# A hybrid decoder step with 64 routed experts: the row lists of the passes turned inside their tiles, and the weights of the last three passes asked for in another order

## The reference

```
scores = sigmoid(h @ w_router)                      # 64 experts in 8 groups
eidx   = the 8 best experts out of the 4 best groups, per row
w      = scores[eidx] / sum * 2.5
routed = sum over the 8 experts e of a row:  w_e * ( silu(h @ w_gate_e) * (h @ w_up_e) ) @ w_down_e
shared = (silu(h @ w_gate_sh) * (h @ w_up_sh)) @ w_down_sh
x      = x + routed + shared,   then a final norm
```

## Time and profile before

| what | value |
|---|---|
| time, median of 3 runs (lowest to highest) | 1099.09 us (1098.98 to 1101.42) |
| the profiled execution | 1099.3 us, of which the span shown by the profile is 1097.5 us |
| PE busy | 934.3 us, 85% of the span |
| PE weight loads busy | 440.3 us, 40% |
| DVE, ACT, POOL busy | 404.1, 202.2, 242.0 us (37%, 18%, 22%) |
| bytes moved by DMA | 289.66 MB, 264 GB/s over the span |
| mean granted TensorE clock | 0.946 of full speed |

### The profile page before, as it was taken

One profiled execution on the slowest core, in us unless ns is written; L12 is line 12 of the kernel. 1 busy time (PEld: TensorE's weight loads), 2 busy tenths in 40 slices (PEclk: granted clock), 3 DMA queues, 4 the chain that ended last, 5 costly groups with the idle time before them and its releaser, 6 DMA issues.

```text
span 1097.5 us, 13692 instructions
## 1 busy us (share of the span) xinstructions
PE 934.3 (85%) x4773; PEld 440.3 (40%) x4773; DVE 404.1 (37%) x975; ACT 202.2 (18%) x415; POOL 242.0 (22%) x301
## 2 busy tenths in 40 slices
PE   4979987997988889799899897899797979999784
PEld 3564555465534544333333332333232324333231
DVE  5957447857873652123111111111111111111116
ACT  6050031141213131111111110111110111111103
POOL 1910029002300166102111211112111210222012
PEclk9989998998999899899899998999898999999988
DMA  9720120231226118899999999999999999999945
GB/s 325 304 77 5 74 78 0 77 90 70 47 79 231 46 55 346 359 377 385 394 381 384 385 389 392 376 381 374 370 394 382 372 374 376 359 339 388 381 147 195
DMA packets 66421, 289.66 MB, mean 264 GB/s; under 512 B 17291, under 2 KB 18539, under 8 KB 41392
## 3 DMA queue, kind: packets, MB, share of 16 engines
q1 hardware_dynamic: 45376, 250.21, 57.7%
q0 software_dynamic: 13232, 35.04, 12.2%
q10 hardware_dynamic: 7744, 3.53, 1.2%
HBM read 257.14 MB, written 41.18 MB: 272 GB/s over the span
## 4 chain that ended last, share of the span: by engine, by line
PE 47%; issue 29%; DVE 13%; ACT 5%; DMA 4%; ACTq 1%; SPq 0%; POOL 0%; DVEq 0%; POOLq 0%
PE bank L998 24%; PE bank L1944 21%; DVE arena L1592 3%; DVE arena L698 2%; PE bank L1036 2%; DMA prm<-expert_lists 1%; DVE arena L800 1%; ACT arena L1265 1%; DMA sum_rows<-arena,xs 1%; ACT arena L1252 1%; DVE bb L720 1%; DMA qkv_samples<-arena 1%; DVE arena L1923 1%; DMA arena<-in_x_prompt 1%; DVE arena L1905 1%
## 5 line engine op out<-in xcount | busy, mean ns | idle before, releaser
L998 PE MATMUL bank<-arena 128*32 128x512 f32 (+6 forms) x2930 | 539.7, 601 | 82.2 <-issue 52.9
L998 PEld LDWEIGHTS bank<-arena 128*32 128x32 f32 (+3 forms) x2930 | 198.3, 132 | 391.1 <-issue 376.4
L1944 PE MATMUL bank<-arena 128*128 128x512 f32 (+9 forms) x1208 | 309.2, 444 | 32.7 <-ACT arena L1549 8.5
L1944 PEld LDWEIGHTS bank<-arena 128*128 128x128 f32 (+4 forms) x1208 | 173.0, 191 | 162.3 <-issue 128.8
L465 POOL DMA_INDIRECT arena<-h_rows,xs x42 | 43.6, 1039 | 466.7 <-DVE bb L720 455.3
L698 DVE SCALAR_TENSOR_TENSOR arena<-arena,xs,bank 128x256 f32<-128x256 f32 x42 | 27.7, 660 | 312.1 <-issue 271.5
L695 DVE COPY arena<-bank 128x512 f32<-128x512 f32 x41 | 28.4, 692 | 179.1 <-PE bank L998 174.6
L554 ACT ACTIVATE arena<-bank 128x256 f32<-128x256 f32 x42 | 16.1, 383 | 328.7 <-PE bank L998 284.2
L474 POOL DMA_INDIRECT sum_rows<-arena,xs x41 | 64.6, 1576 | 53.4 <-DVE arena L695 30.6
L1592 DVE TENSOR_TENSOR arena<-arena 64x512 f32<-64x512 f32 (+8 forms) x79 | 68.3, 865 | 6.5 <-DMA arena<-o_samples 3.8
L484 POOL DMA_INDIRECT expert_lists<-arena,ncim x40 | 39.8, 994 | 91.4 <-issue 87.7
(11 more groups left out here) (231 smaller groups left out, 529.1 us busy)
## 6 DMA issues: line engine op xcount, KB each, us to landing
arena<-in_w_gate_e SPq DMA_DIRECT2D x64, 1024.0 KB, 18.4
arena<-in_w_up_e SPq DMA_DIRECT2D x64, 1024.0 KB, 34.5
arena<-in_w_down_e SPq DMA_DIRECT2D x64, 1024.0 KB, 33.8
arena<-in_w_in SPq DMA_DIRECT2D x5, 2048.0 KB, 9.0
expert_lists<-arena SPq DMA_DIRECT2D x1, 8482.5 KB, 28.9
arena<-in_x_prompt SPq DMA_DIRECT2D x8, 512.0 KB, 5.9
arena<-in_w_out SPq DMA_DIRECT2D x2, 2048.0 KB, 8.3
arena<-sum_rows SPq DMA_DIRECT2D x8, 512.0 KB, 7.9
```

The source lines that it names most:

```text
L998: return nc.tensor.matmul(o, l, r, start=start, stop=stop, skip_group_check=True)
L1944: return nc.tensor.matmul(o, l, r, start=start, stop=stop, skip_group_check=True, **kw)
```

## The change

Four things are changed.

- `segments` joins neighbouring pieces of one list, and `turned` turns each piece of 64 rows or more by `k` rows inside its place in the tile, from pass 4 on: the first entries of the list go to row `c0 + k` and the rows after it, the last `k` to row `c0`. `k` is 16 more than the rest of 5n divided by 16, where n counts the pieces; where that rest is 0 the piece isn't turned. So a turned piece comes as two DMAs, of `width - k` and of `k` rows. The table of row numbers (`c_unit`) is made to match.
- Lists are asked for six passes ahead in place of four (`AHEAD`). Those of passes 4 and 5 are asked for before the first pass.
- The weights of the last three passes (two visits each) are issued by `sync_pair`: both gates, both ups, both downs. The waits for the two places come first, together.
- The last pass projects on gate alone, then on up alone into another PSUM bank (`pe_up_last`), and waits for the ups only before the second; the silu can start in between.

```diff
+ENDING = 3
+AHEAD = 6
+def segments(u):
+    parts = []
+    for r, c0, width, first in UNITS[u]:
+        if parts and parts[-1][0] == r and parts[-1][3] + parts[-1][2] == first:
+            parts[-1] = (r, parts[-1][1], parts[-1][2] + width, parts[-1][3])
+        else:
+            parts.append((r, c0, width, first))
+    return parts
+def turned(u):
+    parts = []
+    for n, (r, c0, width, first) in enumerate(segments(u)):
+        k = 5 * (SEGMENTS_BEFORE[u] + n) % 16 if u >= LISTS and width >= 64 else 0
+        k += 16 if k else 0
+        parts.append((r, c0 + k, width - k, first))
+        if k:
+            parts.append((r, c0, k, first + width - k))
+    return parts
...
-    return 16 * sum(len(UNITS[w]) for w in range(u % LISTS, u + 1, LISTS))
+    return 16 * sum(len(turned(w)) for w in range(u % LISTS, u + 1, LISTS))
...
-            for r, c0, width, first in UNITS[u]:
-                e = act.value_load(order_i[0:1, r:r + 1], min_val=0, max_val=NE - 1)
+            e, known = None, None
+            for r, c0, width, first in turned(u):
+                if r != known:
+                    e, known = act.value_load(order_i[0:1, r:r + 1], min_val=0, max_val=NE - 1), r
                 act.dma_start(lists[u % META][c0:c0 + width, :],
...
+        def sync_pair(sp, u):
+            two = [VISIT_OF[t[0]] for t in UNITS[u]]
+            ids = [sp.value_load(order_i[0:1, VISITS[v_]:VISITS[v_] + 1], min_val=0, max_val=NE - 1) for v_ in two]
+            for v_ in two:
+                sp.wait_ge(s("pe_gu"), NT + pe_free(v_))
+            for kind in range(2):
+                for v_, e in zip(two, ids):
+                    load_one(sp, slot_of(v_), e, kind, "w_last" if u == NU - 1 and kind == 1 else f"w_gu{slot_of(v_)}")
+            for v_ in two:
+                sp.wait_ge(s("pe_down"), NT + pe_free(v_))
+            for v_, e in zip(two, ids):
+                load_down(sp, slot_of(v_), e, f"w_d{slot_of(v_)}")
...
-            if u + LISTS < NU:
-                act_list(act, u + LISTS)
+            if u + AHEAD < NU:
+                act_list(act, u + AHEAD)
...
             act_rows(act, 0)
+            for u in range(LISTS, AHEAD):
+                act_list(act, u)
...
+        def pe_up_last(pe):
+            u = NU - 1
...
+            for kind, out in enumerate((bank[(2, 6)[u % 2]], bank[7])):
+                for v_, cols in tiles_of(u):
+                    if kind == 0:
+                        pe.wait_ge(s(f"w_gu{slot_of(v_)}"), 32 * (v_ // NSLOT) + 16)
+                if kind == 1:
+                    pe.wait_ge(s("w_last"), 32)
+                for k in range(KD):
+                    for v_, cols in tiles_of(u):
+                        t = mmul(out[cols, 0:FE], xgT[u % 2][:, k, cols], gate_up(slot_of(v_))[:, k, kind], k == 0, k == KD - 1)
+                t.then_inc(s("pe_gu"), 1)
```

More of the change, by code:

```diff
@@ L133 @@
 ACCS = make_accumulators()
+def segments(u):
[6 more added lines that the diff above has]
+    return parts
+SEGMENTS_BEFORE = [sum(len(segments(w)) for w in range(u)) for u in range(NU)]
+def turned(u):
[7 more added lines that the diff above has]
+    return parts
 def lists_landed(u):
-    return 16 * sum(len(UNITS[w]) for w in range(u % LISTS, u + 1, LISTS))
+    return 16 * sum(len(turned(w)) for w in range(u % LISTS, u + 1, LISTS))
 def kernel_program(nc, ins, outs):
@@ L365, in load_gate_up, with load_one @@
         def load_gate_up(sp, slot, e, signal):
-            for kind, nm in enumerate(("w_gate_e", "w_up_e")):
-                sp.dma_start(wexp[slot][:, 2048 * kind:2048 * (kind + 1)],
-                             ins[nm][0, bass.ds(e, 1)].rearrange("a (p k) f -> p (a k f)", p=P)).then_inc(s(signal), 16)
+            for kind in range(2):
+                load_one(sp, slot, e, kind, signal)
+        def load_one(sp, slot, e, kind, signal):
+            sp.dma_start(wexp[slot][:, 2048 * kind:2048 * (kind + 1)],
+                         ins[("w_gate_e", "w_up_e")[kind]][0, bass.ds(e, 1)].rearrange("a (p k) f -> p (a k f)", p=P)
+                         ).then_inc(s(signal), 16)
         def load_down(sp, slot, e, signal):
@@ L408, in moe_sync @@
             sp.wait_ge(s("pe_down"), NT)
-            for v_ in range(5, NE):
+            for v_ in range(5, NE - 2 * ENDING):
                 sync_weights(sp, v_)
+            for u in range(NU - ENDING, NU):
+                sync_pair(sp, u)
             sp.wait_ge(s("pe_down"), NT + NU - 1)
@@ L695, in dve_down, with gated @@
             nc.vector.tensor_copy(ys[u % 2][:, 512:1024], bank[5][:, :]).then_inc(s("d_ys"), 1)
-        def gated(b, gate_col, gu):
+        def gated(b, gate_col, up):
             return nc.vector.scalar_tensor_tensor(
                 actg[b].rearrange("t (k p) -> t p k", k=2), sil[b].rearrange("t (p k) -> t p k", k=2), gate_col,
-                gu[:, FE:].rearrange("t (p k) -> t p k", k=2), ALU.mult, ALU.mult)
+                up.rearrange("t (p k) -> t p k", k=2), ALU.mult, ALU.mult)
         def dve_unit(dve, u):
@@ L705, in dve_unit @@
                 dve.wait_ge(s("pe_at"), NT + u - 1)
-            gated(u % 2, gate[:, u % IDX:u % IDX + 1], bank[(2, 6)[u % 2]]).then_inc(s("act_done"), 1)
+            if u == NU - 1:
+                dve.wait_ge(s("pe_gu"), NT + NU + 1)
+            gated(u % 2, gate[:, u % IDX:u % IDX + 1], bank[7][:, 0:FE] if u == NU - 1 else bank[(2, 6)[u % 2]][:, FE:]).then_inc(s("act_done"), 1)
             if u + 1 < NU:
@@ L791, in dve_more @@
             dve.wait_ge(s("ov_act"), 5 * k + 3)
-            gated(0, gate_o, bank[2]).then_inc(s("ov_dve"), 1)
+            gated(0, gate_o, bank[2][:, FE:]).then_inc(s("ov_dve"), 1)
             dve.wait_ge(s("ov_dve"), 4 * k + 3)
@@ L1029, in pe_up @@
             t.then_inc(s("pe_gu"), 1)
+        def pe_up_last(pe):
+            u = NU - 1
+            pe.wait_ge(s("a_xgt"), u + 1)
+            pe.wait_ge(s("d_xgt"), u + 1)
+            pe.wait_ge(s("act_done"), NT + u - 1)
+            for kind, out in enumerate((bank[(2, 6)[u % 2]], bank[7])):
[8 more added lines that the diff above has]
+                t.then_inc(s("pe_gu"), 1)
         def pe_act(pe, u):
@@ L1220, in moe_pe @@
             for u in range(NU):
-                pe_up(pe, u)
+                if u < NU - 1:
+                    pe_up(pe, u)
+                else:
+                    pe_up_last(pe)
                 if u == 4:
@@ L2241, in shape_constants @@
     for u, tiles in enumerate(UNITS):
+        for r_, c0, width, first in turned(u):
+            unit[c0:c0 + width, u] = first + np.arange(width)
         for r_, c0, width, first in tiles:
-            unit[c0:c0 + width, u] = first + np.arange(width)
             unit[c0:c0 + width, 64 + u] = TT * ACCS[u][r_] - FAR
```

## The result

The changed kernel takes 1139.97 us (median of 4 runs, 1133.28 to 1147.28) against 1099.03 us for the kernel before in the same session. The ratio is 1.038 (95% interval 1.033 to 1.042): 41 us slower.

What follows compares the result with a forecast made beforehand. It saw PE busy 85% and DMA engines full mid-run, with PE waiting for weights. From 1099.3 us, +71 late lists, +15 clock, -59 weights, -0.4 silu gave 1126, stated as 1125; range 1084 to 1158, forecast's own 1105 to 1150.

Steps and rivals of the forecast that it cites:

- Equal shares: List DMAs: each is cut equally over engines, a prime row count going to one engine; 7048 packets in ACT's queue.
- 0.30 us a row, each behind a weight packet: Most loaded DMA engine: list rows alternate with weight packets, so four runs of passes need 126, 134, 111 and 122 us.
- rival of rows in bunches: List DMAs: an engine takes several list rows at each turn, so nothing is late; 1087 us, chance 0.08.
- Late lists, +71: Passes 5-9, 14-18, 23-26, 34-38: lists land late and PE stands, +71 us.
- half of 142: Share taken of the upper end for late lists, 35, 43, 33 and 31 us, 142 in all: 71 us.
- the four runs of passes named: Passes 5 to 9, 14 to 18, 23 to 26 and 34 to 38, forecast late by 35, 43, 33 and 31 us.
- ACT's issue is held: ACT's list issues: held behind a full queue, silu and copies wait too; 52 us more, about 1165 us, chance 0.13.
- Clock, +15: PE's projections behind long waits: two waits per late run, eight projections at 1.9 us more for the lower clock, +15 us.
- Weights, -59: Gate and up projections: weights are there first while lists hold PE, giving back 39.6 us of waits and 19 of clock.
- The end, -6 by itself: Last three passes: new weight order and gates first save 6 us by itself, counted within the -59.
- The turn, -8: Gathers and scatters: turning pieces evens out part of the engines' loads, saving 8 us.
- the rival of parts in time: List parts: with shares rounded up, lists land at about 6 us and only gains stay; 1085 us, chance 0.22.

Runs made afterwards that it cites:

- the end alone: Kernel before, with only the new order of the last weights and the gates-first last pass; lists as before: 1095.69 us, ratio 0.997.
- the test of load: To the kernel with turns by multiples of 4, SP adds a DMA of 47 unused list rows in 37 passes: 1098.07 us; with 48 rows: 1080.16 us.

## Why the prediction was right, and where it was not

The forecast was 1125 us and slower, the result 1139.97, inside the range and inside the forecast's own 1105 to 1150. The cause forecast, list rows piled up on one engine behind weight packets, is the right one. The way from there to PE was not, so that the sum came this near is in part luck.

- *Equal shares.* Right: 7048 packets.
- *0.30 us a row, each behind a weight packet.* Right: 43 list packets beside 43.1 weight packets, 0.37 us for each (16 / 43). The rival of rows in bunches falls with it.
- *Late lists, +71.* The step that was mis-sized and put in the wrong place. PE stood 89.4 us more, within the 0 to 142 given; that half of 142 was taken rested on an argument, not on a row. PE stood not where the long lists are used but where ACT issues the next ones. The stands are in passes 2, 9, 11, 13, 18, 21, 29 and 30, counted from 0 by their L1107 groups; ahead of pass p, ACT issues the list of pass p + 5: 7, 14, 16, 18, 23, 26, 34, 35, each in one of the four runs of passes named. (Passes 9 and 18 lie in such runs themselves, but there too PE waited for the product.) DVE hardly waited for a list (1.3 us in all). That is the rival "ACT's issue is held", which I had at 0.13. Its time was wrong: I put its 52 us on top of late lists. As I read it now, the rows that ACT waits out in the issue are those that DVE would have waited for, so that the two do not add.
- *Clock, +15.* Right in size: eight stands, each followed by projections of 12.2 to 13.2 us in place of 10.5 to 10.7, make about 15. That they were eight, two for each of four runs of passes, is luck: by the lists that ACT issued, the four runs had one, three, two and two.
- *Weights, -59.* Right: the projections' waits fell by 41.0 (39.6 forecast), and PE's busy time stayed at 934, so what the lower clock had cost behind the waits for weights about makes up for what it costs behind the new stands.
- *The end, -6 by itself.* 3.4 measured, interval 1.2 to 5.6.
- *Missing.* That rows on few engines slow the weights, or SP, even when no list is late: 18 to 20 us in three experiments, 9 to 17 us of it as longer waits of PE for weights (64.9 against 48.0, 52.6 against 37.8, and 55.4 from SP against 46.2 with the parts cut for 16 engines). In the changed kernel it does not show, since no projection waits over 0.7 us for weights there.
- *The turn, -8 in the rival of parts in time.* 8.4 measured with the parts shared out.

## What to carry to other kernels

Before a transfer's row count is changed, divide it: from SP's and ACT's queues a prime number of rows ran on one engine, and under a full stream of large transfers each of its rows waited for one large packet here. Look at what stands behind the issuing instruction on its engine, because the issue itself can be held, for up to 20 us here; asking six passes ahead did not keep ACT from it. Rows that a gather and a scatter leave out should wander over the tile, in parts that still share out.

## What was not expected of the hardware

- A list DMA of ACT or SP held its engine for 20 to 25 us in the issue (20.16 on ACT, 24.83 in place, 21.96 on SP). How many rows go into the queue before that was not measured; with up to 36 in a pass nothing was held.
- One more row on the loaded engine cost 0.024 us where lists stood there (20.2 us for 836 rows more, 1138 against 302 in passes 4 to 41, with the parts for three or four engines, against the end alone) and 0.011 in the test of load (17.9 us for 1628). Why they differ is open.
- Moving the empty rows of a tile is worth up to 19 us, the largest gain of any part here; that it evens the loads of the gathers and scatters is argued, not shown, since the trace does not tell the engines apart.
